# Dense feed-forward gate and up from step 3 on: seven block products in place of eight

## The reference, cut to what matters

```python
def swiglu(h, w_gate, w_up, w_down):
    return (jax.nn.silu(h @ w_gate) * (h @ w_up)) @ w_down
```

## Time and profile before

| | |
|---|---|
| median of 3 runs | 2551.01 us (2549.07 to 2554.03) |
| profiled execution | 2547.77 us, span 2546.0 us |
| TensorE matmul, weight load | 2469.6 us, 2117.7 us busy |
| VectorE, ScalarE, GpSimd | 475.3, 292.9, 68.3 us busy |
| granted TensorE clock, mean | 0.995 of 2.4 GHz |
| moved by DMA | 584.94 MB |

### The profile page before, as it was taken

One profiled execution on the slowest core, in us unless ns is written; L12 is line 12 of the kernel. 1 busy time (PEld: TensorE's weight loads), 2 busy tenths in 40 slices (PEclk: granted clock), 3 DMA queues, 4 the chain that ended last, 5 costly groups with the idle time before them and its releaser, 6 DMA issues.

```text
span 2546.0 us, 66630 instructions
## 1 busy us (share of the span) xinstructions
PE 2469.6 (97%) x30418; PEld 2117.7 (83%) x30418; DVE 475.3 (19%) x987; ACT 292.9 (12%) x686; POOL 68.3 (3%) x134
## 2 busy tenths in 40 slices
PE   8899999999999999999999999999999999999998
PEld 7787777889999999999999787788777887788775
DVE  1310003520110101101010223331000224331001
ACT  1200001400000000000000123400000123400000
POOL 5000000000000000000000000000000000000000
PEclk9999999989999999999999999999999999999999
DMA  7344444499999999999999544244444553245441
GB/s 224 100 149 149 152 159 154 147 366 394 383 394 394 394 394 394 395 395 394 394 394 392 178 143 150 84 133 146 152 148 148 158 179 107 84 133 162 159 150 66
DMA packets 347688, 584.94 MB, mean 230 GB/s; under 512 B 13508, under 2 KB 187784, under 8 KB 347608
## 3 DMA queue, kind: packets, MB, share of 16 engines
q1 hardware_dynamic: 341400, 581.00, 64.4%
q10 hardware_dynamic: 5728, 2.27, 0.3%
q0 software_dynamic: 480, 0.50, 0.2%
HBM read 582.69 MB, written 1.05 MB: 229 GB/s over the span
## 4 chain that ended last, share of the span: by engine, by line
PE 87%; DMA 8%; ACT 2%; DVE 1%; issue 1%; POOL 0%; ACTq 0%; DVEq 0%; SPq 0%; POOLq 0%
PE ps L746 18%; PE ps L837 16%; PE ps L645 13%; PE ps L757 8%; PE ps L852 7%; PE ps L635 7%; DMA weight_ring<-in_moe_w_up 4%; DMA weight_ring<-in_moe_w_gate 4%; PE ps L723 4%; PE ps L684 2%; PE ps L677 2%; PE ps L773 1%; PE ps L900 1%; PE ps L627 1%; PE ps L863 1%
## 5 line engine op out<-in xcount | busy, mean ns | idle before, releaser
L837 PE MATMUL ps<-heads_feat,weight_ring 128*64 128x84 f32 x14336 | 541.2, 237 | 8.4 <-DMA weight_ring<-in_moe_w_gate 5.1
L837 PEld LDWEIGHTS ps<-heads_feat,weight_ring 128*64 128x64 f32 x14336 | 525.8, 137 | 19.9 <-issue 14.9
L746 PE MATMUL ps<-h_feat,weight_ring 128*128 128x256 f32 x2112 | 461.2, 379 | 0.0
L746 PEld LDWEIGHTS ps<-h_feat,weight_ring 128*128 128x128 f32 x2112 | 401.1, 190 | 67.2 <-issue 14.3
L852 PE MATMUL ps<-scores,weight_ring 128*64 128x84 f32 x7168 | 276.3, 237 | 3.0 <-issue 0.3
L852 PEld LDWEIGHTS ps<-scores,weight_ring 128*64 128x64 f32 x7168 | 265.1, 137 | 11.1 <-issue 11.0
L645 PE MATMUL ps<-h_feat,weight_ring 128*128 128x256 f32 x1152 | 257.2, 382 | 2.1 <-ACT probs_feat L1280 2.0
L645 PEld LDWEIGHTS ps<-h_feat,weight_ring 128*128 128x128 f32 x1152 | 217.8, 191 | 35.1 <-issue 4.9
L1637 DVE SCALAR_TENSOR_TENSOR gelu_tmp<-gelu_tmp,ps 128x336 f32<-128x336 f32 (+1 forms) x92 | 53.0, 576 | 973.2 <-ACT gelu_tmp L1333 518.5
L757 PE MATMUL ps<-weight_ring,scores 128*128 128x512 f32 x480 | 210.9, 592 | 0.0
L635 PE MATMUL ps<-weight_ring,h_feat 128*128 128x256 f32 x864 | 187.9, 379 | 0.6 <-ACT heads_feat L1280 0.6
(11 more groups left out here) (273 smaller groups left out, 1426.2 us busy)
## 6 DMA issues: line engine op xcount, KB each, us to landing
weight_ring<-in_moe_w_gate SPq DMA_DIRECT2D x112, 1024.0 KB, 10.5
weight_ring<-in_moe_w_down SPq DMA_DIRECT2D x112, 1024.0 KB, 11.4
weight_ring<-in_moe_w_up SPq DMA_DIRECT2D x104, 1024.0 KB, 11.3
weight_ring<-in_w_ffn SPq DMA_DIRECT2D x66, 1024.0 KB, 5.3
weight_ring<-in_w_in SPq DMA_DIRECT2D x30, 1024.0 KB, 5.4
weight_ring<-in_w_merge SPq DMA_DIRECT2D x24, 1024.0 KB, 5.2
weight_ring<-in_ffn_w_gate SPq DMA_DIRECT2D x14, 1024.0 KB, 5.0
weight_ring<-in_ffn_w_up SPq DMA_DIRECT2D x14, 1024.0 KB, 5.0
```

What stands on the lines that cost most here:

```text
L746: mm = pe.matmul(bank[:, m * n:(m + 1) * n], w[:, k, m * P:(m + 1) * P], rhs[:, k, :], start=(k == 0), stop=(k == KT - 1))
L837: mm = pe.matmul(out_[c:c + 64], w[:, k, m * P + c:m * P + c + 64], hcur[:, 4 * j + k, :], start=(j == 0 and m % each == 0 and k == 0), st ...
```

## The change

It concerns gate and up of all steps from the third on (s = 2) in the three dense feed-forwards. Each of the two products of a step, 256 features x 256 tokens over a contraction of 1024, is taken as a product of 2 x 2 blocks: the contraction is halved (j: k-tiles 0 to 3 and 4 to 7), the features (i) and the tokens (l). The eight block products become seven, by Strassen's scheme in Winograd's form, with sums of blocks ahead of them and behind. With W_ji and h_jl for the blocks:

- token sums, once per feed-forward, `HS`: S0 = h01 - h00, S1 = h11 - S0, S2 = h11 - h01, S3 = h10 - S1
- weight sums, for each gate and up slot, `WS`: V0 = W01 + W11, V1 = V0 - W00, V2 = W00 - W01, V3 = W10 - V1
- products: P0 = W00 h00, P1 = W10 h10, P2 = W11 S3, P3 = V0 S0, P4 = V1 S1, P5 = V3 h11, P6 = V2 S2
- output: (0,0) = P0 + P1; with Q = P0 + P4 and R = Q + P3: (1,0) = Q + P6 + P2, (0,1) = R + P5, (1,1) = R + P6

VectorE makes all the sums. TensorE's products have 128 tokens and four k-tiles each and are issued as halves of 64 weight columns; four of them fill one bank (P0 to P3) and three the next (P4 to P6), gate in banks 0 and 1, up in 2 and 3, in every step. ScalarE copies them to SBUF (`PR`), 512 columns after the fourth product and 384 after the seventh, VectorE combines them into `GU`, and tanh, `AA` and `HB` then read `GU` in place of PSUM. The buffers lie in parts of `proj` (PJ) and `merge_gates` (SG).

```diff
         ps = ctx.enter_context(nc.psum_tensor("ps", [P, 8, 512], F32))
+        WS = PJ[:, 0:4096].rearrange("p (b m k n) -> p b m k n", b=2, m=4, k=4)
+        HS = PJ[:, 4096:6144].rearrange("p (m k n) -> p m k n", m=4, k=4)
+        PR = (PJ[:, 6144:7680], SG[:, 1024:2560])
+        GU = SG[:, 2560:3584].rearrange("p (b c) -> p b c", b=2)
         selcur = TT[:, 2720:2720 + TT_ * CAP].rearrange("p (t c) -> p t c", t=TT_)
...
         held = [PT[:, :, :].rearrange("p a n -> p (a n)"), ST[:, 2048:4096]] + [
...
                         elif c == 3:
...
-            steps_done, experts_done = [0], [0]
+            steps_done, experts_done, seven_done, calls = [0], [0], [0], [0]
...
                             mm = pe.matmul(bank[:, m * n:(m + 1) * n], w[:, k, m * P:(m + 1) * P], rhs[:, k, :],
...
                     mm.then_inc(sem("slots_used" + over), 1)
+            def seven(q, s, rounds, z, ready):
+                for b, name in ((0, "gate_copied"), (1, "up_copied")):
+                    w = landed(q + b, rounds).rearrange("p (j k i n) -> p j k i n", j=2, k=4, i=2)
+                    if b == 1:
+                        pe.wait_ge(sem("hidden_ready"), ready)
+                    pe.wait_ge(sem(name), z * 2 + 2)
+                    for n, (lhs, rhs) in enumerate((
+                            (w[:, 0, :, 0, :], hT[:, 0:4, 0:P]), (w[:, 1, :, 0, :], hT[:, 4:8, 0:P]),
+                            (w[:, 1, :, 1, :], HS[:, 3, :, :]), (WS[:, b, 0, :, :], HS[:, 0, :, :]),
+                            (WS[:, b, 1, :, :], HS[:, 1, :, :]), (WS[:, b, 3, :, :], hT[:, 4:8, P:2 * P]),
+                            (WS[:, b, 2, :, :], HS[:, 2, :, :]))):
+                        if n == 3:
+                            pe.wait_ge(sem("weights_summed"), z * 2 + b + 1)
+                        out_ = ps[:, 2 * b + n // 4, n % 4 * P:(n % 4 + 1) * P]
+                        for k in range(4):
+                            for c in (0, 64):
+                                mm = pe.matmul(out_[c:c + 64], lhs[:, k, c:c + 64], rhs[:, k, :],
+                                               start=(n % 4 == 0 and k == 0), stop=(k == 3), skip_group_check=True)
+                        if n == 3:
+                            mm.then_inc(sem("products_half_full"), 1)
+                    mm.then_inc(sem("slots_used"), 1)
...
                     pe.wait_ge(sem("ffn_out"), y0)
                 down(q0 + 4, 0, 0, a0 + 1, True, False)
+                z0 = seven_done[0] - 2
+                pe.wait_ge(sem("hidden_ready"), a0 + 1)
+                calls[0] += 1
+                pe.wait_ge(sem("tokens_summed"), calls[0])
                 with pe.Fori(0, (steps - 3) // 2) as i:
...
                         s = 2 + j
-                        gate_up(q0 + 3 * s - 1, s, i, a0 + s - 1 + i * 2)
+                        seven(q0 + 3 * s - 1, s, i, z0 + s + i * 2, a0 + s + i * 2)
                         down(q0 + 3 * s + 1, s - 1, i, a0 + s + i * 2, False, False)
                 for s in range(2 + (steps - 3) // 2 * 2, steps):
-                    gate_up(q0 + 3 * s - 1, s, 0, a0 + s - 1)
+                    seven(q0 + 3 * s - 1, s, 0, z0 + s, a0 + s)
                     if s < steps - 1:
...
                 steps_done[0] += steps
+                seven_done[0] += steps - 2
                 experts_done[0] += 1
             def moe():
...
                 sum_squares(1)
...
-            steps_done = [0]
+            steps_done, seven_done = [0], [0]
+            def products(b, q, z):
+                name = ("gate_copied", "up_copied")[b]
+                if b == 1:
+                    act.wait_ge(sem("up_combined"), z + 1)
+                act.wait_ge(sem("products_half_full"), z * 2 + b + 1)
+                copy(PR[b][:, 0:512], ps[:, 2 * b, :]).then_inc(sem(name), 1)
+                act.wait_ge(sem("slots_used"), q + 1 + b)
+                copy(PR[b][:, 512:896], ps[:, 2 * b + 1, 0:384]).then_inc(sem(name), 1)
+            def seven(s, q, z, ready):
+                products(0, q, z)
+                act.wait_ge(sem("gate_combined"), z + 1)
+                act.wait_ge(sem("gate_ready"), ready)
+                act.activation(TH[:, s % 2, :], GU[:, 0, :], ACT.Tanh, scale=0.5).then_inc(sem("tanh_ready"), 1)
+                products(1, q, z)
...
                 q0, a0 = SLOT[name], steps_done[0]
...
                 step(1, q0 + 2, a0 if a0 else None)
-                with act.Fori(0, (steps - 2) // 2) as i:
+                z0 = seven_done[0] - 2
+                with act.Fori(0, (steps - 3) // 2) as i:
                     for j in range(2):
                         s = 2 + j
-                        step(s, q0 + 3 * s - 1 + i * 6, a0 + s - 1 + i * 2)
-                for s in range(2 + (steps - 2) // 2 * 2, steps):
-                    step(s, q0 + 3 * s - 1, a0 + s - 1)
+                        seven(s, q0 + 3 * s - 1 + i * 6, z0 + s + i * 2, a0 + s - 1 + i * 2)
+                for s in range(2 + (steps - 3) // 2 * 2, steps):
+                    seven(s, q0 + 3 * s - 1, z0 + s, a0 + s - 1)
                 steps_done[0] += steps
+                seven_done[0] += steps - 2
...
                 q0 = SLOT["moe"]
...
                     y_half(1, scale).then_inc(sem("out_added"), 1)
...
-            steps_done, outs_done = [0], [0]
+            steps_done, outs_done, seven_done = [0], [0], [0]
+            def token_sums():
+                dve.wait_ge(sem("dve_drained"), n_job[0])
+                h = hT[:, :, :].rearrange("p (j k) (l n) -> p j k l n", j=2, l=2)
+                link(tt(HS[:, 0, :, :], h[:, 0, :, 1, :], h[:, 0, :, 0, :], ALU.subtract))
+                link(tt(HS[:, 1, :, :], h[:, 1, :, 1, :], HS[:, 0, :, :], ALU.subtract))
+                tt(HS[:, 2, :, :], h[:, 1, :, 1, :], h[:, 0, :, 1, :], ALU.subtract)
+                tt(HS[:, 3, :, :], h[:, 1, :, 0, :], HS[:, 1, :, :], ALU.subtract).then_inc(sem("tokens_summed"), 1)
+            def weight_sums(b, q, rounds, z):
+                n = z * 4 + 2 * b
+                dve.wait_ge(sem(f"slot_in{q % SLOTS}"), rounds * 16 + 16 * (q // SLOTS + 1))
+                w = w_slot(q).rearrange("p (j k i n) -> p j k i n", j=2, k=4, i=2)
+                tt(WS[:, b, 0, :, :], w[:, 0, :, 1, :], w[:, 1, :, 1, :], ALU.add).then_inc(sem("weights_linked"), 1)
+                tt(WS[:, b, 2, :, :], w[:, 0, :, 0, :], w[:, 0, :, 1, :], ALU.subtract)
+                dve.wait_ge(sem("weights_linked"), n + 1)
+                tt(WS[:, b, 1, :, :], WS[:, b, 0, :, :], w[:, 0, :, 0, :], ALU.subtract).then_inc(sem("weights_linked"), 1)
+                dve.wait_ge(sem("weights_linked"), n + 2)
+                tt(WS[:, b, 3, :, :], w[:, 1, :, 0, :], WS[:, b, 1, :, :], ALU.subtract).then_inc(sem("weights_summed"), 1)
+            def combined(b, z):
+                n = z * 4 + 2 * b
+                dve.wait_ge(sem(("gate_copied", "up_copied")[b]), z * 2 + 4)
+                pr = PR[b].rearrange("p (a n) -> p a n", n=P)
+                by_three = PR[b].rearrange("p (a n) -> p a n", n=3 * P)[:, :, 0:P]
+                o = GU[:, b, :].rearrange("p (i l n) -> p i l n", i=2, l=2)
+                tt(pr[:, 7, :], pr[:, 0, :], pr[:, 4, :], ALU.add).then_inc(sem("products_linked"), 1)
+                dve.wait_ge(sem("products_linked"), n + 1)
+                tt(pr[:, 8:10, :], pr[:, 7:8, :].to_broadcast([P, 2, P]), by_three[:, 1:3, :], ALU.add).then_inc(
+                    sem("products_linked"), 1)
+                dve.wait_ge(sem("products_linked"), n + 2)
+                tt(o[:, :, 0, :], by_three[:, 0:4:3, :], pr[:, 1:3, :], ALU.add)
+                tt(o[:, :, 1, :], pr[:, 8:9, :].to_broadcast([P, 2, P]), pr[:, 5:7, :], ALU.add).then_inc(
+                    sem(("gate_combined", "up_combined")[b]), 1)
+            def seven(s, q, rounds, z, done, more):
+                p = s % 2
+                combined(0, z)
+                if more:
+                    weight_sums(0, q + 3, rounds, z + 1)
+                dve.wait_ge(sem("tanh_ready"), done + 1)
+                stt(AA[:, p, :], TH[:, p, :], 1.0, GU[:, 0, :], ALU.add, ALU.mult).then_inc(sem("gate_ready"), 1)
+                combined(1, z)
+                dve.wait_ge(sem("gate_ready"), done + 1)
+                dve.wait_ge(sem("up_combined"), z + 2)
+                tt(HB[:, p, :, :].rearrange("p f t -> p (f t)"), AA[:, p, :], GU[:, 1, :], ALU.mult).then_inc(
+                    sem("hidden_ready"), 1)
+                if more:
+                    weight_sums(1, q + 4, rounds, z + 1)
...
                 q0, a0 = SLOT[name], steps_done[0]
+                if not a0:
+                    dve.engine_nop().then_inc(sem("gate_copied"), 2)
+                    dve.engine_nop().then_inc(sem("up_copied"), 2)
+                    dve.engine_nop().then_inc(sem("up_combined"), 1)
+                z0 = seven_done[0] - 2
+                token_sums()
+                weight_sums(0, q0 + 5, 0, z0 + 2)
                 step(0, q0, a0)
```

(10 more changed lines are left out.)

## The result

The changed kernel takes 2515.4 us (median of 4 runs, 2513.6 to 2516.7) against 2550.0 us before (4 runs): the ratio is 0.9861, with a 95% interval from 0.9844 to 0.9878, or 34.7 us less. The forecast was 2513 in a range of 2502 to 2530.

What follows compares the result with a forecast made beforehand. TensorE alone was taken to bound the kernel. A step of 12.23 (products) + 0.35 (turns) + 6.87 (down) = 19.45 us saves 1.23; 30 steps save 36.9 us, giving 2510.9 or 2514.1, stated as 2513, range 2502 to 2530.

Steps and rivals of the forecast that it cites:

- Thirty steps, TensorE alone: Dense feed-forwards: 12 + 9 + 9 = 30 steps change, each worth exactly what its matmuls take on TensorE.
- 109.2 ns a pair: Gate and up: 112 pairs of half-array records at 128 columns, 109.2 ns each, 12.23 us a step.
- Turns of 0.35 us: TensorE going to halves before the gate products and back to the full array for down: 0.35 us a step together.
- The step: One changed feed-forward step: 12.23 + 0.35 + 6.87 = 19.45 us, 1.23 us less than 20.68.
- Cover of VectorE and ScalarE: Sums, copies and combinations within a step: about 10.3 us VectorE, 2.8 us ScalarE, hidden behind TensorE at zero cost.
- The end: Each feed-forward's end: last hidden ready 3.1 us after the last product, fitting before down_last's ninth record by about 0.5 us.
- The sum: Whole kernel: 30 x 1.23 = 36.9 us less, 2510.9 from the profiled execution or 2514.1 from the median, stated as 2513.
- The range: Whole kernel: terms at their bounds span gains of 25 to 40 us, 2508 to 2526 (77%), widened to 2502 to 2530.
- Busy time of the narrow records: Gate and up in the changed kernel: 6720 narrow records with a busy time near 30 x 12.5 = 375 us.
- The dearer stream of short matmuls: Gate and up: about 81 ns per 128-column matmul, over 17 us a step, over 100 us lost; stronger form of a 4% rival.

Runs made afterwards that it cites:

- down_halves: Changed kernel with every down also issued as halves of 64 stationary columns, so the loop never turns between shapes: 2507.6 us, ratio 0.9825 to the kernel before.
- eight_blocks: Kernel before, gate and up from step 2 on as eight block products of 128 tokens in halves of 64 weight columns, no sums: 2565.9 us, ratio 1.0055.
- old_halves: Kernel before, gate and up from step 2 on as halves of 64 weight columns, still 256 tokens, down on the full array: 2564.0 us, ratio 1.0044.
- the kernel with two additions: Changed kernel with two unused VectorE additions of 2048 elements ahead of each slot's weight sums: 2515.6 us, ratio 0.986 to the kernel before.

## Why the prediction was right

- **Thirty steps, TensorE alone.** Right. No row of the changed kernel's steps has TensorE waiting.
- **109.2 ns a pair.** Right to the digit: (12.38 - 0.15) / 112 = 109.2. down_halves gives it without a turn to subtract (12.23 / 112), and eight_blocks gives 109.1 with 128 pairs.
- **Turns of 0.35 us.** 0.34: 0.15 before the down and 0.19 at it, in the changed kernel as in old_halves, gone in down_halves. The bound of 0.5 for a first record of 512 columns wasn't needed: it lost as much as one of 256 columns. A sum without them would have missed by 30 x 0.34 = 10.2 us. The Trainium skill's rule that a change of tiling mode drains TensorE (TensorEngine Tiling (Array Packing), section Tiling Modes) agrees with this: each change has a price, and none is paid where both neighbours have halves. That the price is a drain, no run shows.
- **The step.** 19.44 us measured, 19.45 forecast; gain 1.24 against 1.23.
- **Cover of VectorE and ScalarE.** Right and shown, with the first wait at the place named. It came only with VectorE's step above TensorE's. In the changed kernel the sums for the gate of the next step are ready 11.1 us before the fourth product, those for its up 10.4 us (10.5 and some 10 by the forecast). VectorE's step is 9.24 us, not 10.3: two neighbouring operations without a wait between them start 0.60 to 0.61 us apart where one takes 0.69, which the sum had counted in full. Its total, 719, is below the 740 named for the same reason; ScalarE's 359 is as said.
- **The end.** 2.98 us from the last product to the last hidden, forecast 3.1; 0.4 us of cover, forecast about 0.5.
- **The sum.** The feed-forwards gave 37.1 us against 36.9. The kernel gave 34.7 by the medians. The step missed no term. The profiled pair has its difference in stages that the change doesn't touch, part of it by the clock; for the 2.4 us between the traces and the medians that is likely but not shown. The same holds for the 3.2 us between the profiled execution and the median of before, which I had split; the new median of before is 1.0 us lower, and the forecast's 2513 is 2.4 us below the result.
- **The range.** One sum in it is wrong. With every term at its bound the step gains 20.68 - 12.51 - 0.5 - 6.87 = 0.80 us, and the kernel 30 x 0.80 - 1.5 = 22.5 us, not 25. The inner range should have ended at 2528.5 and not at 2526, which is still inside the stated 2530.
- **Busy time of the narrow records.** I had named 375 us. The groups of L771 add up to 419 us, since their modelled ends overlap those of the next group; the chain's 30 x 12.38 = 371 is the number to compare. That was a wrong view for a right quantity.
- **The dearer stream of short matmuls** did not come: a record takes 109.2 ns in halves and 111.7 on the full array. At 0.834 ns a column, two cycles of 2.4 GHz, that is two passes of 55 or 56 ns. The Trainium skill's 81 ns a matmul (TensorE: Matmul & The Clock Gate, section Back-to-back issue gap) is not seen here in any form.
- **Not tried:** a version that also takes step 1 in seven products. It would need gate and up banks that step 0 still holds.

## What to carry to other kernels

When one engine alone makes the chain, price a change in that engine's own records, taken at the new shape from anywhere in the trace, and then count the places where the shape changes: here 60 turns cost a fifth of what the fewer products gave, and issuing the untouched neighbour in the new shape got nearly all of it back. Cover is best given as a number of microseconds with its place, since it can then be tested by adding work until it breaks. Two covers that an engine has in one step are the same idle time and don't add up, and a lead counts only from the last point at which that engine had to wait for the other: here VectorE stood idle for 12.9 us at the head of the loop with and without the extra work in front of it, so nothing was saved up and nothing was spent.

## What the runs showed that was not expected

- A turn costs on both sides, and not only as a gap: the record behind the first one is late too. In the changed kernel the second record of a down starts 0.53 us after the first, where the others are 0.43 apart; the down is 0.19 us longer in all.
- Halves of 64 weight columns are cheaper than the full array at 128 moving columns (109.2 against 111.7 ns) and equal at 512 (6.87 us for a down in both forms). With no turns around them they are the better form, and with two turns a step the worse.
- TensorE's granted clock fell for a short stretch in the compressed attention of the second block, in the first of its layers in every execution that was profiled. The projection of 64 records there takes 14.02 us at full clock and took up to 17.02 (in the kernel with two additions, second layer). Those 3 us are 0.1% of the kernel, so a change of that size has to be read from the chain of its own stage and not from the span. What makes the clock fall here stays open.
